# Clearing a stage's semaphores by ranges of neighbouring numbers in a two-layer hybrid trunk

## The chip, the cores and the metric

One core of one Trainium2 chip runs the whole program. The metric is the device time in microseconds, 4389.47 us as the median of 3 runs (4385.0 to 4389.6). The profiled execution was a further one.

## What is computed

The reference is a trunk of DEPTH = 2 layers over 256 latent and 256 context tokens of width 1024, in f32. Cut to its frame, one layer is:

```
mod_l = silu(c) @ w_mod[l] + b_mod[l]
hl = rmsnorm(x, norm1_w[l]) * (1 + sc1) + sh1
pl_ssd, pl_rwkv, pl_na, pl_gate = split(hl @ w_in[l])
ya, yb, yc = ssd_mixer(...), rwkv_mixer(...), na_mixer(...)
x = x + g1 * merge_branches((ya, yb, yc), pl_gate, w_branch[l], w_out[l])
toks = rmsnorm(x, norm2_w[l]) * (1 + sc2) + sh2
x = x + g2 * moe_ffn(toks, route_hierarchical(toks, ...), ...)   # 4 groups of 4 experts, top 2
```

The context tokens go through the same weights; in the second layer (l = 1) they are only read. A last rmsnorm gives the output, 256 x 1024. The change touches none of this arithmetic: it touches the semaphores between the stages.

## The kernel before, in words

The program is a chain of 21 stages, each written by hand as one block with a program for every engine: PE (TensorE), DVE (VectorE), ACT (ScalarE), POOL (GpSimd) and SP (SyncE, which issues nearly all DMAs). Activations stay in SBUF, channels on the partitions and tokens in the free dimension, 512 tokens in layer 0 and mostly the 256 latent ones in layer 1. Each layer runs, in this order, `modulation` (w_mod streamed through five buffers), `conv_project` (z/x/B/C projection and convolution), `ssd_mix`, `branch_streams` (z, attention, two merges), `rwkv_heads`, `residual_out` (w_out), `norm_tokens`, `route`, `experts_rows` (layer 0) or `experts` (layer 1), and `experts_dense` (runs only when a token found no slot, so here it reads a flag and ends). `finish` closes the program.

A block ends in a barrier of all engines: each engine drains and adds to a semaphore, POOL collects them and lets all five go on. A stage's semaphores come from the context manager `phase` (L164), entered ahead of the block, so its end stands behind the block's barrier. There SP alone clears them, one `sem_clear` each (L170), and there is no barrier after that. The numbers go back to the allocator one stage later, when another barrier lies between (L171 to 173). So the other engines go straight into the next stage, and SP goes into it behind its clears. SP's clears are in front of whatever SP does first in the next stage:

- `conv_project` (L516, L517): two small DMAs, then `take_first_slabs`.
- `branch_streams` and `residual_out`: `take_first_slabs` at once. It waits for the two weight slabs that the stage before had already asked for (the ring holds two slabs of 2 MB) and then hands each on by an increment (L229). PE's first matmul (L264 in `multiply_slabs`, L1014 in `branch_streams`) waits for that increment and not for the DMA itself.
- `modulation` (L301): the first DMA of w_mod.
- `rwkv_heads` (L1444, L1445, L1440): the weights of the low-rank terms and of the next turn; PE itself starts on weights that an earlier stage loaded (L1480).
- `norm_tokens`: the first six DMAs of the experts' down weights. `route`, `experts_rows`, `experts`, `experts_dense`, `finish` and `ssd_mix`: SP first waits for something that the stage works out later, or does nothing.

Two places have a second barrier. At the end of each layer's experts the stage's semaphores are cleared, then 19 (layer 0) or 14 (layer 1) semaphores of the weight stream one by one (L2908), and then all engines meet in a barrier (L2909). At the very end 15 long-lived semaphores are cleared (L2913) ahead of the last barrier (L2914).

The numbers are handed out in ascending order, from the one behind the last given, from 255 on to 114, and past those still held. In the program before, the stages have these (the number of semaphores, then the ranges):

```
layer 0                              layer 1
modulation     22  114-135           modulation     22  214-235
conv_project    6  136-141           conv_project    6  236-241
ssd_mix        30  142-171           ssd_mix        30  114-129, 242-255
branch_streams 43  172-214           branch_streams 43  130-148, 164-187
rwkv_heads     76  114-148, 215-255  rwkv_heads     76  149-163, 188-248
residual_out    6  168-173           residual_out    6  121-126
norm_tokens     5  174-178           norm_tokens     5  127-131
route           9  179-187           route           9  132-140
experts_rows    9  188-196           experts        13  141-148, 168-172
experts_dense  17  197-213           experts_dense  17  166-167, 173-187
                                     finish          7  159-165
```

That is 457 semaphores in 27 ranges over the 21 stages.

Of the kernel before, what the change touches and what calls it, by code (L numbers as in the profile page):

```python
# [162 lines left out]
@contextmanager  # L163
def phase(nc, names):  # L164

    _phase[0] += 1
    sems = namedtuple("Semaphores", names)(*(nc.alloc_semaphore(name=f"{n}_{_phase[0]}") for n in names.split()))
    yield sems
    for s in sems:
        nc.sync.sem_clear(s)  # L170
    for s in _cleared:  # L171
        nc.release_semaphore(s)
    _cleared[:] = sems
# [96 lines left out]
def modulation(k):  # L270
# [4 lines left out]
    NR = 5  # L275
    with ExitStack() as st:
        s = st.enter_context(phase(nc, " ".join(f"slab{i}" for i in range(NR)) + " slab_free rows_done rows_in turned rows_free padded silu_c small rest vec "
                               "tokens updated square summed mean normed affine"))
        sc = st.enter_context(nc.sbuf_tensor(f"silu_c{l}", [P, KT, 32], F32))
# [136 lines left out]
def norm_tokens(k, t0, *cleared):  # L416

    nc, l = k.nc, k.layer
    n = TT - t0
    with ExitStack() as st:  # L420
        s = st.enter_context(phase(nc, "sum root scaled moved cleared"))
        rinv = st.enter_context(nc.sbuf_tensor(f"rinv_second{l}", [P, TT], F32))
        block = st.enter_context(nc.Block())
# [32 lines left out]
def residual_out(k, t0):  # L456

    nc, l = k.nc, k.layer
    with ExitStack() as st:
        s = st.enter_context(phase(nc, STREAM + " updated square summed"))  # L460
        sq = st.enter_context(nc.sbuf_tensor(f"sq_out{l}", [P, 2, TT], F32))
        block = st.enter_context(nc.Block())
# [2504 lines left out]
```

How the kernel before makes its waits and increments, by code:

```python
    def settle(self):  # L147
        self.eng.wait_ge(self.sem, self.base + self.n)
# [37 lines left out]
def inverse_root(k, act, rinv, sums, done):  # L186
    k.nc.scalar.activation(rinv, sums, ACT.Ln, scale=1.0 / D, bias=const(k, "eps")).then_inc(done, 1)
    act.wait_ge(done, 1)
    k.nc.scalar.activation(rinv, rinv, ACT.Exp, scale=-0.5).then_inc(done, 1)
# [26 lines left out]
def take_first_slabs(k, sp, loaded, amount):  # L217
    plan = k.plans.pop(0)
    if not k.asked:
        for h in range(2):
            for dst, src in slab_parts(k, plan, h):
                sp.dma_start(dst, src).then_inc(k.first[h], 16)
    k.n_first += 16 * len(slab_parts(k, plan, 0))
    k.asked = False
    for h in range(2):
        sp.wait_ge(k.first[h], k.n_first)
        sp.sem_inc(loaded[h], amount)
# [2 lines left out]
def ask_next_slabs(k, sp, frees):  # L232
    if not k.plans:
        return
    for h in range(2):
        sp.wait_ge(*frees[h])
        for dst, src in slab_parts(k, k.plans[0], h):
            sp.dma_start(dst, src).then_inc(k.first[h], 16)
    k.asked = True
# [2 lines left out]
def load_slabs(k, sp, s, w, col0, turns):  # L243
    wv = w.rearrange("(kt p) c -> p kt c", p=P)
    loaded = (s.loaded0, s.loaded1)
    take_first_slabs(k, sp, loaded, 16)
    for n in range(2, 2 * turns):
        sp.wait_ge(s.tile_done, 4 * (n - 1))
        sp.dma_start(k.ring[:, n % 2], wv[:, :, col0 + 512 * n:col0 + 512 * n + 512]).then_inc(loaded[n % 2], 16)
    ask_next_slabs(k, sp, [(s.tile_done, 8 * turns - 4), (s.tile_done, 8 * turns)])
```

## Time and profile before

| | us |
|---|---|
| median of 3 runs | 4389.47 |
| lowest and highest run | 4385.0, 4389.6 |
| profiled execution, its time | 4385.84 |
| profiled execution, first to last instruction (span) | 4384.1 |

In the profile PE is busy for 4005.9 us of the span (91%), DVE for 1383.7 (32%), ACT for 1013.4 (23%) and POOL for 455.3 (10%). "Busy" leaves out register, semaphore and DMA-issuing instructions; those stand as an engine's queue (SPq, PEq and so on). SP has no busy time at all and is seen only in its queue. Each row of work gives the idle time ahead of it on its engine and, behind an arrow, what ended that idle time. All times below count from the span's start.

### The profile page before, as it was taken

To read this page: it belongs to the slowest core of one execution; us is meant where nothing else is said; L and a number is where in the kernel's file an instruction comes from. 1 tells how busy PE (TensorE), PEld (TensorE's weight loads), DVE (VectorE), ACT (ScalarE), POOL (GpSimd) and SP (SyncE) were. 2 spreads that over 40 slices of the span, in tenths; PEclk is the share of its full clock that TensorE was granted. 3 is DMA by queue.
4 is the path that set the end of the run, shared out by engine and by line. 5 is a ranking of instruction groups with operands and counts; after the bars stand their busy time and mean duration, and the time that the engine had idled before them with its cause. 6 is when DMAs were issued, how large, how long until landed. Compare 5 with 4: busy or idle time off the path is not lost. (4 is left out here: it accounts for less than half of the span.)

```text
span 4384.1 us, 94494 instructions
## 1 busy us (share of the span) xinstructions
PE 4005.9 (91%) x42596; PEld 2712.0 (62%) x42596; DVE 1383.7 (32%) x2784; ACT 1013.4 (23%) x1735; POOL 455.3 (10%) x360
## 2 busy tenths in 40 slices
PE   5999998999999999879999588998999999998996
PEld 2454445448887785368878235656678887874332
DVE  1471004235555461110000145202255555512111
ACT  2121005124343331100000122103143443311101
POOL 0050002101111110000000002102011111100000
PEclk8999999999999999979999798999999999998998
DMA  7201222220000011349998631223201000146996
GB/s 306 77 1 58 86 62 64 96 57 19 19 19 19 21 42 40 140 166 315 324 309 285 247 136 39 87 77 106 79 19 35 19 19 21 42 138 255 404 403 269
DMA packets 299414, 539.20 MB, mean 123 GB/s; under 512 B 52320, under 2 KB 160112, under 8 KB 298880
## 3 DMA queue, kind: packets, MB, share of 16 engines
q1 hardware_dynamic: 291392, 505.80, 33.4%
q0 software_dynamic: 7616, 27.27, 1.7%
q8 instruction: 342, 5.60, 0.5%
q14 instruction: 64, 0.52, 0.0%
HBM read 515.13 MB, written 17.87 MB: 122 GB/s over the span
## 5 line engine op out<-in xcount | busy, mean ns | idle before, releaser
L1470 PE MATMUL bank<-inv 64*64 64x64 f32 x15104 | 487.9, 219 | 19.0 <-ACT inv L1793 8.5
L1470 PEld LDWEIGHTS bank<-inv 64*64 64x64 f32 x15104 | 467.4, 135 | 56.5 <-issue 54.7
L1014 PE MATMUL bank<-sb_h,sb_ring 128*128 128x512 f32 (+1 forms) x1344 | 480.4, 517 | 14.3 <-DMA sb_ring<-w_branch 7.0
L1014 PEld LDWEIGHTS bank<-sb_h,sb_ring 128*128 128x128 f32 x1344 | 257.8, 193 | 230.2 <-issue 198.3
L2665 PEld LDWEIGHTS bank<-xs,gu 128*128 128x128 f32 x3072 | 347.3, 193 | 8.6 <-issue 7.4
L2665 PE MATMUL bank<-xs,gu 128*128 128x96 f32 x3072 | 347.3, 276 | 1.0 <-DVE hid L2594 1.0
L1480 PE MATMUL bank<-sb_h,sb_ring 128*128 128x512 f32 (+1 forms) x672 | 276.8, 566 | 6.2 <-DMA sb_ring<-w_in 4.1
L264 PE MATMUL bank<-sb_h,sb_ring 128*128 128x512 f32 x512 | 224.7, 602 | 17.4 <-SPq L229 17.4
L1480 PEld LDWEIGHTS bank<-sb_h,sb_ring 128*128 128x128 f32 x672 | 128.7, 193 | 138.5 <-issue 129.3
L264 PEld LDWEIGHTS bank<-sb_h,sb_ring 128*128 128x128 f32 x512 | 98.8, 193 | 141.7 <-issue 124.2
L2490 PE MATMUL bank<-gu,xs 128*64 128x512 f32 x768 | 169.8, 594 | 9.0 <-DMA gu<-moe_w_up 8.5
L1014 PE MATMUL bank<-sb_branch,sb_ring 128*128 128x512 f32 (+1 forms) x512 | 170.5, 486 | 0.0
L2677 PE MATMUL bank<-sb_ring,hid 128*96 128x512 f32 x384 | 167.5, 592 | 1.2 <-issue 1.2
L2593 DVE TENSOR_TENSOR hid<-hid,bank 128x192 f32<-128x192 f32 x16 | 5.7, 355 | 510.9 <-ACT hid L2629 510.9
L1793 ACT ACTIVATE inv<-bank 128x512 f32<-128x512 f32 x192 | 111.3, 596 | 155.9 <-PE bank L1470 155.9
L1237 DVE TENSOR_TENSOR sb_acc<-zs,bank 128x512 f32<-128x512 f32 (+1 forms) x16 | 8.9, 554 | 430.5 <-PE bank L1014 430.5
L1014 PEld LDWEIGHTS bank<-sb_branch,sb_ring 128*128 128x128 f32 x512 | 97.1, 190 | 69.3 <-issue 61.2
L363 PE MATMUL bank<-mod_ring,silu_c 128*32 128x512 f32 x384 | 68.2, 847 | 69.2 <-DMA mod_ring<-w_mod 69.2
L2490 PEld LDWEIGHTS bank<-gu,xs 128*64 128x64 f32 x768 | 53.5, 137 | 119.6 <-issue 99.7
L2677 PEld LDWEIGHTS bank<-sb_ring,hid 128*96 128x96 f32 x384 | 61.3, 163 | 95.7 <-issue 95.7
L1470 PE MATMUL bank<-cc,bb 64*64 64x128 f32 x2048 | 118.7, 269 | 0.1
L1086 PE MATMUL bank<-vtok,pt 128*128 128x64 f32 x640 | 86.2, 275 | 30.6 <-DVE sb_branch L1277 23.3
(391 smaller groups left out, 5939.6 us busy)
## 6 DMA issues: line engine op xcount, KB each, us to landing
mod_ring<-w_mod SPq DMA_DIRECT2D x24, 2048.0 KB, 22.7
sb_ring<-w_in SPq DMA_DIRECT2D x24, 2048.0 KB, 7.8
gu<-moe_w_gate SPq DMA_DIRECT2D x128, 384.0 KB, 8.7
gu<-moe_w_up SPq DMA_DIRECT2D x128, 384.0 KB, 10.0
sb_ring<-moe_w_down SPq DMA_DIRECT2D x96, 512.0 KB, 4.5
gu<-moe_w_gate SPq DMA_DIRECT2D x64, 768.0 KB, 14.0
gu<-moe_w_up SPq DMA_DIRECT2D x64, 768.0 KB, 14.9
sb_ring<-moe_w_down SPq DMA_DIRECT2D x32, 1024.0 KB, 14.8
```

The source lines that it names most:

```text
L264: mm = nc.tensor.matmul(banks[j], ring[:, h, kt, P * j:P * j + P], rhs[:, kt], start=kt == 0, stop=kt == KT - 1)
L363: mm = nc.tensor.matmul(k.bank[1 + j % 4][32 * g:32 * g + 32], sc[:, 4 * hf + g], ring[:, n % NR, g, 512 * i:512 * i + 512], start=hf == 0 ...
L1014: mm = nc.tensor.matmul(out, left(kt), right(kt), start=kt == 0, stop=kt == KT - 1)
L1086: mm = nc.tensor.matmul(Y[u % 2][:, 64 * h:64 * h + 64], pt[:, j % 3, t], vtok[:, t, P * f + 64 * h:P * f + 64 * h + 64], start=t == 0, st ...
L1237: tt(k.acc[:, t, t0:], sg[:, t % 2, t0:], projs[0][t % 2][:, 0:n], ALU.mult).then_inc(s.merged, 1)
L1470: m = mm(bank[hs, at:at + w], left(hs), right(hs), start=start, stop=True, skip_group_check=True)
L1480: m = mm(k.bank[RAW_BANK[j]][:, WHOLE[j]:], w[:, j, kt], k.h[:, kt, WHOLE[j]:], start=kt == 0, stop=kt == KT - 1)
L1793: ac(slot(z, into), eight(k.bank[2 + 3 * z + j]), ACT.Copy).then_inc(s.ev_a, 1)
L2490: m = mm(wide[i][rows[e], :], xs[:, kt, rows[e]], cols[:, 512 * i:512 * i + 512], start=kt == 0, stop=kt == KT - 1)
L2593: nc.vector.tensor_tensor(h[:, 0:2 * C], h[:, 0:2 * C], wide[1][:, 2 * C:4 * C], ALU.mult)
L2665: m = mm(wide[j // 4][:, C * (j % 4):C * (j % 4) + C], w[:, P * j:P * j + P], xs[:, kt], start=kt == 0 and j % 4 == 0, stop=kt == KT - 1, ...
L2677: m = mm(outs[half][0:C], hid[:, r % 2, f], ws.down[d % ws.n_down][:, 0, 512 * half:512 * half + 512], start=f == 0, stop=f == HT - 1)
```

## The change

When a stage ends, its semaphores' numbers are sorted, split into runs of neighbouring numbers, and each run is cleared by one `sem_clear` with a range. Nothing else is changed: the same engine clears, at the same place, and numbers are released as before. The clears at L2908 and L2913 stay one by one.

```diff
     yield sems
-    for s in sems:
-        nc.sync.sem_clear(s)
+    numbers = sorted(s.num for s in sems)
+    for i, a in enumerate(numbers):
+        if i == 0 or numbers[i - 1] + 1 < a:
+            first = a
+        if i + 1 == len(numbers) or a + 1 < numbers[i + 1]:
+            nc.sync.sem_clear(range(first, a + 1))
     for s in _cleared:
         nc.release_semaphore(s)
     _cleared[:] = sems
```

## Rows read from the trace of the kernel before

**Rows 1.** Who waited for whom: us in total, times, longest us.

```profile
PE bank L363 <- DMA mod_ring<-w_mod: 69.2, 24, 16.8
PE bank L264 <- SPq L229: 29.7, 4, 8.9
PE bank L1014 <- SPq L229: 5.9, 2, 3.2
...
SPq L2811 <- DVE sb_h L2845: 11.5, 4, 9.5
```

**Rows 2.** Line 170: count, ns min/median/max, first and last start; whole, then stretches.

```profile
L170 SPq EVENT_SEMAPHORE_RANGE_CLEAR  x457: 25/30/49, 88.7 to 4382.9; - x153
...
L170 SPq EVENT_SEMAPHORE_RANGE_CLEAR  x76: 25/28/30, 3919.8 to 3924.1; - x76
...
L170 SPq EVENT_SEMAPHORE_RANGE_CLEAR  x76: 25/30/37, 1784.6 to 1789.4; - x76
...
L170 SPq EVENT_SEMAPHORE_RANGE_CLEAR  x30: 25/30/49, 338.2 to 340.4; - x30
...
L170 SPq EVENT_SEMAPHORE_RANGE_CLEAR  x22: 25/30/39, 88.7 to 90.0; - x22
```

**Rows 3.** Timeline into conv_project: start us, us, engine, line [idle before <-releaser].

```profile
90.05 0.37 SPq L516 DMA_DIRECT2D wdt<-w_in  x1
90.47 0.57 SPq L517 DMA_DIRECT2D dtpar<-dt_par  x1
...
91.15 1.22 PE L264 MATMUL bank<-sb_h,sb_ring 128*128 128x512 f32 x1 [8.44 <-SPq L229]
```

**Rows 4.** Timeline into residual_out of layer 0.

```profile
1783.67 0.69 DVE L2154 TENSOR_TENSOR sb_acc<-sb_acc,bkt 128x512 f32<-128x512 f32 x1
...
1789.48 2.93 PE L264 MATMUL bank<-sb_acc,sb_ring 128*128 128x512 f32 x3 [6.64 <-SPq L229]
...
1790.83 0.37 SPq L2347 DMA_DIRECT2D wr<-router_w  x1
```

**Rows 5.** GB/s in 40 slices of 1740 to 1800 us, 1.5 us each.

```profile
GB/s 348 197 0 0 0 0 5 0 0 0 0 0 0 0 0 33 371 395 407 193 0 0 0 0 0 0 0 0 0 105 411 390 396 112 38 52 214 395 412 414
```

**Rows 6.** Timeline into branch_streams of layer 0.

```profile
338.24 1.28 ACT L1150 ACT_TABLE_LOAD   x1 [10.03 <-PEq L563]
...
340.52 1.22 PE L1014 MATMUL bank<-sb_h,sb_ring 128*128 128x512 f32 x1 [3.21 <-SPq L229]
```

**Rows 7.** Timeline into modulation of layer 1.

```profile
2472.93 0.93 SPq L301 DMA_DIRECT2D mod_ring<-w_mod  x2
```

**Rows 8.** Line 2909, the barrier behind the experts.

```profile
L2909 DVEq DRAIN  x2: 19/19/19, 2465.2 to 4360.7; - x2
...
L2909 SPq DRAIN  x2: 7/7/7, 2466.7 to 4362.2; - x2
```

**Rows 9.** Timeline into rwkv_heads of layer 0, SP and PE.

```profile
924.88 0.58 SPq L1444 DMA_DIRECT2D sb_ring<-wa  x1
...
922.23 8.80 PE L1480 MATMUL bank<-sb_h,sb_ring 128*128 128x512 f32 x16 [2.02 <-PEq L918]
930.96 0.69 PE L1489 MATMUL bank<-sb_ring 64*128 64x512 f32 x1
```

**Rows 10.** Stretches: us, PE busy (x), PEld, DVE, ACT, POOL, PEclk, DMA share, GB/s.

```profile
340.50:346.70 6.20, 6.18 (x8) 2.58 (x9) 0.00 (x0) 0.00 (x0) 1.25 (x1) 0.50 0.00 0
...
1789.40:1793.90 4.50, 4.42 (x5) 1.85 (x6) 0.00 (x0) 0.00 (x0) 0.00 (x0) 0.50 0.47 75
...
2773.90:2776.90 3.00, 2.97 (x7) 2.44 (x8) 0.00 (x0) 0.00 (x0) 1.77 (x1) 0.50 0.00 0
...
3924.20:3927.20 3.00, 2.96 (x7) 2.43 (x8) 0.00 (x0) 0.00 (x0) 0.00 (x0) 0.50 0.48 178
...
923.50:926.90 3.40, 3.40 (x5) 1.35 (x4) 0.86 (x9) 0.00 (x0) 0.00 (x0) 0.50 0.13 38
```

**Rows 11.** GB/s in 40 slices of 3930 to 4000 us, 1.75 us each.

```profile
GB/s 388 406 410 409 400 402 404 402 400 402 355 25 0 0 0 108 405 396 424 421 410 412 417 405 213 5 0 0 0 0 9 5 0 0 0 0 0 0 49 342
```

## Prediction

> **What bounds the kernel now.** I read the waits first, since PE is busy for 91% of the span and only what moves PE, or what PE waits for, moves the end. In the table of waits PE waits 29.7 us in four places at L264 and 5.9 us in two at L1014 for "SPq L229" [rows 1]. That is SP's increment that hands on a weight slab. Slabs take long to come, so one would expect PE to be waiting for a DMA there. It isn't: in residual_out of layer 0 the transfer rate shows two bursts of about 2 MB, one in slices 15 to 19 (1762 to 1770 us), one in slices 29 to 33 (1783 to 1791) [rows 5]. The first slab was there some 13 us before the stage began. What SP does between the barrier and L229 is to clear: 76 clears from 1784.6 to 1789.4 [rows 2], and PE's first matmul starts at 1789.48 behind 6.64 us of idle time, while the last work of the stage before, on DVE, ended at 1783.67 + 0.69 = 1784.4 [rows 4]. So of the 6.6 us, 4.8 are SP's clears. SP is never "busy" in the page, and still it sets PE's start at six borders.
>
> The other numbers that matter are those of a clear itself. All 457 are already instructions of the range kind, here with a range of one; each is shown for 25 to 49 ns, 30 at the median [rows 2]. From the 76 clears of layer 1 (3919.8 to 3924.1), 4.3 us / 75 = 57 ns from one to the next, so 57 ns is what one costs SP [rows 2]. In layer 0 some runs are longer than that: 4.8 instead of 4.3 us for 76, and 2.2 instead of 29 x 0.057 = 1.7 us for 30 [rows 2], about 1.0 us of stalls in sum, whose cause no row names.
>
> **The change, part by part.** 457 clears become 27, so 430 go, 430 x 0.057 = 24.5 us of SP's time. What counts is where SP is waited for. No instruction is added on any other engine, no wait is added, and what SP is queued up to do comes earlier.
>
> (a) Into conv_project, twice: 22 clears become 1, 21 x 0.057 = 1.2 us each. Behind them SP issues two DMAs (0.37 and 0.57 us) and reaches L229; PE starts at 91.15 [rows 3]. Late next would be the two issues, which stay. 2.4 us.
>
> (b) Into branch_streams, twice: 30 become 1 in layer 0 and 2 in layer 1 (29 + 28) x 0.057 = 3.2 us. PE starts at 340.52, just behind the last clear at 340.4 [rows 2, 6]. ACT's table load, 338.24 to 339.52, doesn't hold PE, and its first copy comes only after a group of matmuls [rows 6].
>
> (c) Into residual_out, twice: 76 become 2, 2 x 74 x 0.057 = 8.4 us, the largest term. Late next in layer 0: SP's wait for the second slab, which lands at 1790.8 whatever SP does (its next issue, at 1790.83, shows it [rows 4]); PE needs it only half way through the stage, behind the four output tiles of the first slab. The rates show that the first slab landed long before [rows 5].
>
> (d) The barrier behind the experts: SP drains at 2466.7, DVE had at 2465.2, so all wait for SP's clears [rows 8]. 9 become 1 and 13 become 2: 19 x 0.057 = 1.1 us. The 19 and 14 stream clears stay.
>
> (e) Into modulation of layer 1: 17 become 1, 16 x 0.057 = 0.9 us. SP's first DMA of w_mod at 2472.93 is behind them [rows 7], and PE waits 69.2 us for these slabs over both layers [rows 1], so the stage is set by the stream and moves with its start.
>
> (f) Ahead of the last barrier 7 become 1: 6 x 0.057 = 0.3 us.
>
> (g) 142 further clears go at no gain. Into rwkv_heads 43 become 1 and 2 (83 in all): SP's first DMA leaves at 924.88, but PE is in 8.80 us of matmuls on weights already there and goes on at 930.96 without a gap [rows 9]; without that cover it would be worth 2.4 us a layer. Into ssd_mix, norm_tokens, route and the experts 44 go, where SP has nothing that anyone waits for at once, and into finish 15, where SP waits for DVE's last line anyway [rows 1]. Were all of this uncovered it would be 142 x 0.057 = 8.1 us; I take 0.
>
> The sum of (a) to (f) is 42 + 57 + 148 + 19 + 16 + 6 = 288 clears, 288 x 0.057 = 16.5 us. Of the 1.0 us of stalls, both on gated borders, between 0 and 1.0 may go with the clears; I take 0.5.
>
> (h) TensorE's clock. Behind these borders PE starts at a granted clock of 0.50, which is 1.2 of 2.4 GHz: 6.2 and 3.0 us into branch_streams, 4.5 and 3.0 us into residual_out [rows 10]. Half speed costs half of that, (6.2 + 4.5 + 3.0 + 3.0) / 2 = 8.3 us in sum. The idle time ahead would shrink from 3.2 to 1.0 us and from 6.6 to 2.0 in layer 0, and alike in layer 1. The nearest row for a short gap is the one into rwkv_heads: 2.02 us idle, and the clock still fell, for 3.4 us, which cost 1.7 [rows 9, 10]. If all four borders came to cost as that one, 8.3 - 6.8 = 1.5 us are won; if none fell, 8.3. For residual_out, whose gaps come nearest to that row, I take its price (3.75 - 3.4 = 0.3 us won); for branch_streams, with gaps of half that length, half of the 4.6 us. Together 2.6 us. Into conv_project the gap stays above 7 us and the clock stays low.
>
> Sum: 16.5 + 0.5 + 2.6 = 19.6 us. Against the profiled execution's own 4385.84 us that gives 4366.2. That execution was 3.6 us below the median of the runs (4389.47), near the lowest of them; against the median it is **4369.9 us**, which I give.
>
> **What a range costs.** The trace has no range of more than one number. Bounded by rows: at the low end a range takes the 57 ns of a single clear whatever its length; at the high end the 30 ns for which a clear is shown are spent once per number, and only the other 27 are saved. I take the low end, because the instruction is the same one and a range of one uses it in full. The Trainium skill speaks for the high end (Runtime: NRT & Kernel Launch, "The ~15µs preamble/postamble breakdown"): the runtime's reset of 51 semaphores per engine is put at about 1.5 us, 29 ns a number, though it doesn't say whether single or ranged clears do it. By that figure, as an estimate, the saving at the gated borders would be about half; no row of this case shows it.
>
> **Rivals.** *A range works through its numbers.* 288 x 0.027 = 7.8 us are won, 4381.7 us. For it: a clear is shown as working for 30 of its 57 ns, and that part would be the one to grow [rows 2]. Against it: nothing in the rows varies with a number. 10%.
>
> *A stream takes the gain back.* The experts of layer 1 live on their weight stream. If it ran through from residual_out on, its start (behind the second slab's landing, which doesn't move) would set the end, and the 4.2 us of that border would be lost: 4374 us. Against it: the rates pause from about 3974 to 3996 us, with the buffers full, until the experts free some [rows 11]; an earlier start just shortens the pause. 6%.
>
> *Slower.* The place is the same borders: if one number inside a range cost more than the 57 ns of a clear of its own, each border would be longer than before. The gated borders hold 302 numbers in 14 ranges. From 57 ns a number it decides; at 90 ns, say, (90 - 57) x 302 = 10 us slower, 4399 us. Nothing in the rows speaks for it. 3%.
>
> That the change doesn't do what it says could come from numbers that aren't neighbours; the table of numbers gives at most two ranges a stage, so no more than a few clears are in doubt. 1%, about no change.
>
> **How the numbers follow.** The forecast holds 80%. A measurement of this kernel can tell about 0.2%, 8.8 us, from no change. Forecast and stream case lie beyond that (86%, and a little of the first rival when clock luck is added), the first rival mostly within. Range: the low end is 16.5 + 1.0 + 8.3 = 25.8 us below the median, 4363.7, less some 2.5 us as the runs before themselves reach 4.5 below theirs: 4361. The high end takes in the first rival: 4382.
>
> **What would show it.** In the changed profile line 174 should have 27 clears; PE's waits for SP's increment should fall from 35.6 us to about 21 (247 of the 288 clears stand there: 35.6 - 14.1 - 0.5), with the first matmul of residual_out under 2.5 us behind the last matmul ahead of it. If a clear of 41 numbers is shown for far more than 30 ns, the first rival is right, above 2.4 us the slower one. If the waits fall as said but the time doesn't, the stream took it, and the experts' waits for DMA grow. If the clock still stands at 0.50 for as long into branch_streams, term (h) was wrong.

## The result, and the profile after

The changed kernel ran in 4363.28 us (median of 4 runs, 4361.85 to 4364.93), beside 4388.43 us for the kernel before in the same comparison. The ratio is 0.9944, 95% interval 0.9927 to 0.9961: 24.6 us faster, between 17 and 32. In a later series of its own (e9 below) the ratio was 0.9961, 0.9947 to 0.9975: 17 us, between 11 and 23. The profiled execution took 4361.85 us, its span was 4360.0. Forecast were 4369.9 us and 19.6 us of gain.

The clears of the changed kernel, line 174, over the whole span and then at some borders (count, ns min/median/max, first and last start in us):

```profile
L174 SPq EVENT_SEMAPHORE_RANGE_CLEAR  x27: 31/49/125, 89.6 to 4358.7; - x27
...
L174 SPq EVENT_SEMAPHORE_RANGE_CLEAR  x1: 68/68/68, 89.6 to 89.6; - x1
L174 SPq EVENT_SEMAPHORE_RANGE_CLEAR  x1: 75/75/75, 337.8 to 337.8; - x1
L174 SPq EVENT_SEMAPHORE_RANGE_CLEAR  x1: 98/98/98, 916.4 to 916.4; - x1
L174 SPq EVENT_SEMAPHORE_RANGE_CLEAR  x2: 83/92/101, 1781.3 to 1781.4; - x2
L174 SPq EVENT_SEMAPHORE_RANGE_CLEAR  x2: 49/87/125, 3903.9 to 3904.0; - x2
L174 SPq EVENT_SEMAPHORE_RANGE_CLEAR  x1: 35/35/35, 208.4 to 208.4; - x1
```

27 clears stand where 457 stood [rows 2]. The rows also tell what a range costs: it is shown for 35 ns with 6 numbers, 68 with 22, 75 with 30 and 98 with 43. From 6 to 43 numbers that is 63 ns more, so 1.7 ns a number, beside the 30 ns for which a clear of one number is shown. By that rate the 302 numbers on the gated borders cost about half a microsecond in sum.

Who waited for whom, PE, in the changed kernel, beside [rows 1]:

```profile
PE bank L268 <- SPq L233: 18.3, 4, 7.4
...
PE bank L2531 <- DMA down<-moe_w_down: 16.9, 13, 1.5
...
PE bank L2494 <- DMA gu<-moe_w_up: 6.8, 8, 1.1
...
PE bank L1018 <- SPq L233: 2.2, 2, 1.1
```

The waits for SP's increment fell from 35.6 to 20.5 us, by 15.1. Of the 18.3 that remain at L268, 14.7 (7.25 and 7.40) are the two borders into conv_project, where PE has been idle since well before the barrier.

The timeline at the borders of layer 0, into conv_project, branch_streams and residual_out, beside [rows 3, 6, 4], and the first DMA of modulation in layer 1, beside [rows 7]:

```profile
89.68 0.37 SPq L520 DMA_DIRECT2D wdt<-w_in  x1
...
90.79 2.08 PE L268 MATMUL bank<-sb_h,sb_ring 128*128 128x512 f32 x2 [7.25 <-SPq L233]
...
337.92 1.56 PE L1018 MATMUL bank<-sb_h,sb_ring 128*128 128x512 f32 x3 [1.08 <-SPq L233]
...
1780.30 0.69 DVE L2158 TENSOR_TENSOR sb_acc<-sb_acc,bkt 128x512 f32<-128x512 f32 x1
...
1781.57 8.85 PE L268 MATMUL bank<-sb_acc,sb_ring 128*128 128x512 f32 x20 [2.11 <-SPq L233]
...
2461.70 1.61 SPq L305 DMA_DIRECT2D mod_ring<-w_mod  x2
```

Into residual_out PE now starts 0.6 us behind DVE's last instruction (1780.99); before it was 5.1 us. And the row, which merges matmuls that follow one another, has changed its look: 20 matmuls in 8.85 us, 0.44 us each, where the first three of before took 2.93 us [rows 4]. That is the clock. Stretches of the changed kernel, the same borders (us, PE busy, PEld, DVE, ACT, POOL, PEclk, DMA share, GB/s), beside [rows 10]:

```profile
337.90:341.00 3.10, 3.08 (x7) 1.44 (x8) 0.00 (x0) 1.15 (x1) 3.10 (x1) 1.00 0.04 8
...
1781.60:1786.00 4.40, 4.40 (x11) 2.01 (x12) 0.00 (x0) 0.00 (x0) 0.00 (x0) 1.00 1.04 399
...
2759.70:2762.70 3.00, 3.00 (x14) 2.66 (x15) 0.00 (x0) 1.01 (x1) 3.00 (x1) 1.00 0.01 3
...
3904.20:3908.00 3.80, 3.77 (x17) 3.34 (x18) 0.01 (x1) 0.00 (x0) 0.00 (x0) 1.00 0.98 370
...
914.50:916.60 2.10, 0.08 (x2) 0.04 (x1) 1.38 (x2) 0.00 (x0) 0.00 (x0) 1.00 0.03 7
916.60:921.00 4.40, 4.40 (x7) 1.95 (x8) 1.94 (x9) 0.00 (x0) 0.00 (x0) 0.63 0.62 161
```

All four borders that began at 0.50 now begin at a granted clock of 1.00. The one into rwkv_heads, whose price was taken for a short gap, fell again (0.63 over the 4.4 us behind it). The span shortened by 4384.1 - 4360.0 = 24.1 us. PE's earlier starts are 15.1 of it, the four half-clock stretches 8.3 (their cost in [rows 10]), which leaves 0.7 for the rest; the barriers and the stream of term (d) to (f) were forecast at 2.3. That rest also holds what two executions differ by anyway.

The neat sum hides larger pieces of both signs. A stage's length can be read from the moment at which one barrier lets DVE go to the moment at which the next one does. Measured so, the two branch_streams and the two residual_out are together 21.9 us shorter (the table below), both conv_project 2.9 us, modulation of layer 1 2.3 us, and the three stretches that end in the barriers behind line 2908 and at the very end 1.2 us. Against that, the two rwkv_heads are 3.5 us longer and ssd_mix of layer 1 2.3 us longer, though the change does nothing inside them. In ssd_mix of layer 1 the same 426 matmuls took longer, at a lower granted clock; before and after:

```profile
2670.90:2772.09 101.19, 83.41 (x426) 60.64 (x426) 61.53 (x101) 18.90 (x32) 31.17 (x24) 0.85 0.02 8
...
2655.86:2759.36 103.50, 86.78 (x426) 62.65 (x426) 61.51 (x101) 18.78 (x32) 31.16 (x24) 0.81 0.02 7
```

PE's busy time over the whole span fell by 5.0 us (4005.9 to 4000.9) and not by 8.3: part of what the clock gives at the four borders was lost elsewhere in this execution. The 8.3 us are the clock's share at those borders, not over the whole program.

### The profile page after: what moved, and what is told of

Same layout as the page of the kernel before. It is cut to its first block and busy times, and to the rows that moved or that the text cites. A ratio compares the mean times of both kernels' runs of the same rounds, so it can differ in the third digit from the quotient of the medians.

```text
span 4360.0 us, 94064 instructions
## 1 busy us (share of the span) xinstructions
PE 4000.9 (92%) x42596; PEld 2710.7 (62%) x42596; DVE 1384.2 (32%) x2784; ACT 1013.2 (23%) x1735; POOL 455.7 (10%) x360
## 5 line engine op out<-in xcount | busy, mean ns | idle before, releaser
L268 PE MATMUL bank<-sb_h,sb_ring 128*128 128x512 f32 x512 | 224.4, 601 | 14.6 <-SPq L233 14.6
L268 PEld LDWEIGHTS bank<-sb_h,sb_ring 128*128 128x128 f32 x512 | 98.7, 193 | 138.9 <-issue 124.1
## 6 DMA issues: line engine op xcount, KB each, us to landing
mod_ring<-w_mod SPq DMA_DIRECT2D x24, 2048.0 KB, 22.4
```

What stands on the lines that cost most here:

```text
L268: mm = nc.tensor.matmul(banks[j], ring[:, h, kt, P * j:P * j + P], rhs[:, kt], start=kt == 0, stop=kt == KT - 1)
```

## The experiments

All ratios are to the kernel before, in the same series. Series of kernel before: 4384.44 us (e1 to e4, 20 runs), 4386.38 us (e5 to e8, 31 runs), 4386.28 us (e9 to e11, 9 runs). Times of one kernel spread over 10 us and more within a series, so that a few microseconds show in a profile's rows before they show in a ratio. The lengths of the four stages behind the borders into branch_streams and residual_out, in us (from barrier to barrier, as above), one profiled execution each:

| kernel | branch_streams, layer 0 | residual_out, layer 0 | branch_streams, layer 1 | residual_out, layer 1 | sum |
|---|---|---|---|---|---|
| before | 583.80 | 65.04 | 387.30 | 35.69 | 1071.8 |
| the change | 578.64 | 58.32 | 382.86 | 30.12 | 1049.9 |
| e2, ranges into residual_out | 583.84 | 58.31 | 386.09 | 30.12 | 1058.4 |
| e3, clears on POOL | 578.54 | 58.07 | 382.68 | 29.88 | 1049.2 |
| e5, PE busy in residual_out | 582.16 | 62.86 | 383.62 | 34.22 | 1062.9 |
| e6, PE busy in all four | 580.77 | 62.86 | 385.24 | 34.22 | 1063.1 |
| e7, 18 clears put back | 579.73 | 61.52 | 386.66 | 32.75 | 1060.7 |
| e8, 36 clears put back | 583.95 | 61.97 | 386.45 | 35.02 | 1067.4 |

Branch_streams of layer 1 is the least steady of them: the kernel of e4 and e10, the same program twice, took 387.83 and 383.18 us there.

**e1, ranges only where nobody waits for SP.**

```diff
-    for s in sems:
-        nc.sync.sem_clear(s)
+    hidden = _phase[0] in (2, 4, 6, 7, 8, 12, 14, 16, 17, 18, 20)
+    if hidden:
+        numbers = sorted(s.num for s in sems)
...
+    else:
+        for s in sems:
+            nc.sync.sem_clear(s)
```

> Ranges only behind the stages after which nobody waits for SP (the 11 borders of term (g): into ssd_mix, rwkv_heads, norm_tokens, route, experts and finish); the 288 clears of the gated borders stay one by one. 142 clears fewer, 8.1 us of SP's time. Theory (what counts is who waits for SP): no change, 0 within 4 us, and PE's waits for SP's increment stay near 35.6 us. Rival (fewer instructions of SP help by themselves, through its fetching or anything else shared): about 142/430 of the 25 us gained, 8 us faster.

Measured: ratio 1.0003, 0.9994 to 1.0012 (4386.79 us), so between 3 us faster and 5 us slower. PE's waits for SP's increment are 35.9 us in its profile (29.3 + 6.6):

```profile
PE bank L273 <- SPq L238: 29.3, 4, 8.6
...
PE bank L1023 <- SPq L238: 6.6, 2, 3.3
```

The rival's 8 us lie outside the interval. 142 clears fewer are worth less than 3 us, and nothing that the waits show, where other work covers them.

**e2, ranges only on the two borders into residual_out.**

```diff
+    if names.startswith("w_in second_in"):
+        numbers = sorted(s.num for s in sems)
...
+    else:
+        for s in sems:
+            nc.sync.sem_clear(s)
```

> Ranges only behind rwkv_heads, that is on the two borders into residual_out, 148 clears fewer. Theory with the clock: 8.5 us for the clears (0.5 of it stalls) and 3.7 us for TensorE's clock, which no longer falls to half behind these borders: 12.2 us faster than before. Rival without the clock: 8.5 us. In the profile PE's first matmul stands 0.4 us behind the barrier and the stage shows no stretch at a clock of 0.50.

Measured: ratio 0.9973, 0.9963 to 0.9983, 11.8 us faster (between 7.5 and 16). The point is the theory's with the clock, 12.2, though 8.5 lies within the interval too. The profile decides: the two residual_out stages are 6.7 and 5.6 us shorter, 12.3 in sum, and PE starts with a full-speed row behind a gap of 2.10 us,

```profile
1785.08 2.41 PE L272 MATMUL bank<-sb_acc,sb_ring 128*128 128x512 f32 x5 [2.10 <-SPq L237]
```

five matmuls in 2.41 us where the kernel before took 2.93 for three [rows 4]. About half of the 24.6 us sits on these two borders.

**e3, the same 457 single clears, issued by POOL.**

```diff
     for s in sems:
-        nc.sync.sem_clear(s)
+        nc.gpsimd.sem_clear(s)
```

> The 457 clears stay one by one, but POOL issues them in place of SP. Theory (SP's place on the path counts, not the number of clears): nearly the whole gain of the change, 23 to 25 us, less about 0.5 us where POOL's gathers in experts_rows now stand behind 9 clears and 1 us at the barriers behind the experts. Rival (the number of clears counts, whoever issues them): no change from before.

Measured: ratio 0.9949, 0.9937 to 0.9960, 22.4 us faster (between 17.5 and 27.6). The clears are all there, line 170, now on POOL and shown for 44 ns each, and PE doesn't wait for them (19.6 us of waits for SP's increment are left, 20.5 in the change; the four stages are as short as there):

```profile
L170 POOLq EVENT_SEMAPHORE_RANGE_CLEAR  x457: 44/44/48, 87.6 to 4365.1; - x153
...
1778.75 1.55 PE L264 MATMUL bank<-sb_acc,sb_ring 128*128 128x512 f32 x3 [1.86 <-SPq L229]
```

So neither the number of clears nor the range as such is the cause of the gain. The cause is that the clears stood in the queue of the engine that lets PE go.

**e4, ranges also for the stream's and the last semaphores.**

```diff
-                for sem in k.stream.sems:
-                    nc.sync.sem_clear(sem)
+                clear(nc, k.stream.sems)
...
-        for sem in (k.dt_in, k.w3_in, *k.first, *k.pool_dma):
-            nc.sync.sem_clear(sem)
+        clear(nc, (k.dt_in, k.w3_in, *k.first, *k.pool_dma))
```

> The changed kernel with the stream's 19 and 14 and the last 15 semaphores cleared by ranges too; 45 clears fewer, all ahead of a barrier at which everyone waits for SP. Theory: 45 x 0.058 = 2.6 us faster than the change, 27 to 28 us faster than before. Rival (a longer range costs with its numbers as much as the clears it replaces): no faster than the change.

Measured: ratio 0.9941, 0.9928 to 0.9953, 25.9 us faster (between 21 and 32). 48 clears became 4 here (44 fewer, not the 45 of the text), 31 in all. The ratios can't tell it from the change; the barriers can. Drains at the barrier behind the experts, DVE and SP, first and last start in us: the change, then this kernel (its execution in e10).

```profile
L2913 DVEq DRAIN  x2: 19/19/19, 2455.2 to 4337.6; - x2
L2913 SPq DRAIN  x2: 7/7/7, 2456.3 to 4338.5; - x2
...
L2916 DVEq DRAIN  x2: 19/19/19, 2457.1 to 4340.1; - x2
L2916 SPq DRAIN  x2: 7/7/7, 2457.2 to 4340.3; - x2
```

SP now drains 0.1 and 0.2 us behind DVE, where it was 1.1 and 0.9 in the change. From barrier to barrier the three closing stretches take 1.25 us in sum in e4 and e10, 3.88 in the change and in e9: 2.6 us less, which is what the theory has.

**e5 and e6, all clears kept, and PE kept busy in the gap.** This takes the clock's share apart from SP's. In e5 the matmuls stand in residual_out alone; e6 adds those of branch_streams.

```diff
         def _(pe):
+            for i in range(5 if t0 == 0 else 9):
+                nc.tensor.matmul(k.bank[7][:, t0:], const(k, "ones"), k.acc[:, i % KT, t0:], start=True, stop=True)
             multiply_slabs(pe, nc, s, k.ring, k.acc[:, :, t0:], banks, 1, s.updated)
...
+            for i in range(2 if t0 == 0 else 3):
+                nc.tensor.matmul(k.bank[7][:, t0:], const(k, "ones"), k.h[:, i, t0:], start=True, stop=True)
             gate_z()
```

> The kernel before with all its clears, and in residual_out PE runs matmuls whose result nobody reads (5 in layer 0, 9 in layer 1, about 4 us) while it waits for SP; they write a bank that the stage doesn't use. SP's path is that of before. Theory (the idle gap lets the clock fall, and that is a loss of its own beside the clears): 3.3 us in layer 0 and 1.7 us in layer 1 won, 4 to 5 us faster than before, with no stretch at 0.50 behind these borders. Rival (the clock is no separate term): no change, or slower by what the matmuls overrun the wait.

> As e5, and in branch_streams too (2 and 3 such matmuls ahead of the first wait). Theory: another 3.4 us in layer 0 and 1.5 us in layer 1, so 8 to 10 us faster than before with every clear in its old place, the clock's whole share of the change's 25 us. Rival: as e5.

Measured: e5 0.9986, 0.9977 to 0.9995, 6.1 us faster (between 2 and 10); e6 0.9980, 0.9971 to 0.9989, 8.8 us faster (between 5 and 13). The timeline of e5 into residual_out of layer 0 and a stretch of it, then stretches of e6 into branch_streams:

```profile
1782.74 4.53 PE L473 MATMUL bank<-sb_acc,sb_consts 128*128 128x512 f32 x10 [1.84 <-PEq L1390]
1787.54 4.99 PE L264 MATMUL bank<-sb_acc,sb_ring 128*128 128x512 f32 x11 [0.27 <-SPq L229]
...
1782.60:1789.40 6.80, 6.39 (x15) 2.72 (x16) 0.00 (x0) 0.00 (x0) 0.00 (x0) 1.00 0.79 297
```

```profile
338.40:345.00 6.60, 6.12 (x14) 2.68 (x15) 0.00 (x0) 1.28 (x1) 3.51 (x1) 1.00 0.02 5
2768.90:2775.00 6.10, 5.79 (x26) 4.83 (x27) 0.09 (x1) 1.67 (x2) 3.51 (x1) 1.00 0.01 4
```

PE waits for SP as long as ever, but with work in hand, and the real matmuls start at full speed. e6 gains 8.8 us without one clear less, which agrees with the 8.3 us of the four half-clock stretches in [rows 10]; its four stages are 8.7 us shorter than before. In e5 the two residual_out stages are 3.7 us shorter, of the 4 to 5 expected.

**e7 and e8, the change with the delay put back in doses.** 18 (e7, shown) or 36 (e8) clears of one already cleared semaphore on the four borders into branch_streams and residual_out.

```diff
             nc.sync.sem_clear(range(first, a + 1))
+    if names.startswith(("w_in second_in", "logits act")):
+        for _ in range(18):
+            nc.sync.sem_clear(sems[0])
```

> The changed kernel with 18 more clears of one already cleared semaphore on the four borders into branch_streams and residual_out. Each such border is 18 x 0.058 = 1.0 us longer. Theory: 4.2 us slower than the change where the clock stays up, and up to 6.8 us more where gaps of 2 to 3 us let it fall; by the gaps (about 2.1 and 2.4 us in branch_streams, 3.1 and 2.4 us in residual_out) I expect the clock to fall in one or two of the four, 6 to 8 us slower. Rival (a clear costs SP nothing that PE sees): no change.

> As e7 with 36 clears, 2.1 us on each of the four borders, gaps of 3.2 to 4.2 us, as long as those of before in branch_streams. Theory: 8.4 us for the clears and the clock falling on all four, 5 to 8 us: 13 to 16 us slower than the change. Rival without the clock: 8.4 us.

Measured: e7 0.9972, 0.9962 to 0.9982 (12.3 us faster than before); e8 0.9978, 0.9969 to 0.9987 (9.6 us). Against the change, whose two series give 24.6 and 17.1 us, that is 5 to 12 and 7 to 15 us slower; the ratios don't separate the theory from its rival, as the change's own spread is too wide. The rows do. In e8 the gaps ahead of the four borders are 8.7 us longer in sum than in the change, and the four stages 17.5 us longer. The rival without the clock has nothing for the other 8.8 us. The whole is a little more than the 13 to 16 us expected. In e7 the gaps are 5.1 us longer and the stages 10.7, where 6 to 8 were expected. Its timeline shows the gap ahead of the four borders (in brackets), and the stretches behind them the clock:

```profile
338.76 1.56 PE L1021 MATMUL bank<-sb_h,sb_ring 128*128 128x512 f32 x3 [2.17 <-SPq L236]
...
1784.06 4.54 PE L271 MATMUL bank<-sb_acc,sb_ring 128*128 128x512 f32 x6 [3.61 <-SPq L236]
...
2764.51 2.07 PE L1021 MATMUL bank<-sb_h,sb_ring 128*128 128x256 f32 x4 [2.60 <-SPq L236]
...
3911.36 2.08 PE L271 MATMUL bank<-sb_acc,sb_ring 128*128 128x256 f32 x4 [2.63 <-SPq L236]
```

```profile
338.70:342.00 3.30, 3.23 (x8) 1.56 (x9) 0.00 (x0) 0.10 (x1) 2.33 (x1) 1.00 0.01 2
1784.00:1789.00 5.00, 4.94 (x8) 2.16 (x9) 0.00 (x0) 0.00 (x0) 0.00 (x0) 0.66 0.75 282
2764.50:2768.00 3.50, 3.49 (x9) 2.84 (x10) 0.00 (x0) 0.00 (x0) 1.84 (x1) 0.55 0.01 2
3911.30:3916.00 4.70, 4.64 (x14) 3.86 (x15) 0.00 (x0) 0.00 (x0) 0.00 (x0) 0.66 0.98 373
```

Behind 2.17 us the clock stayed up (1.00), behind the other three it fell. I had expected one or two to fall. In e8, with gaps of 3.34, 4.24, 3.29 and 3.71 us, all four started low:

```profile
339.10:344.00 4.90, 4.87 (x6) 2.19 (x7) 0.00 (x0) 0.00 (x0) 1.12 (x1) 0.50 0.01 2
1786.00:1790.00 4.00, 3.98 (x6) 1.89 (x7) 0.00 (x0) 0.00 (x0) 0.00 (x0) 0.61 0.74 275
2769.60:2773.00 3.40, 3.40 (x8) 2.78 (x9) 0.00 (x0) 0.00 (x0) 1.13 (x1) 0.50 0.00 0
3916.80:3922.00 5.20, 5.16 (x12) 4.17 (x13) 0.00 (x0) 0.00 (x0) 0.00 (x0) 0.50 0.67 253
```

**e9 to e11, the change, all ranges, and a warm start of conv_project, in one series.** e9 is the change, e10 is e4. e11 adds to e10, at the end of PE's part of modulation:

```diff
             pe.sem_inc(s.turned, 1)
+            for i in range(4):
+                nc.tensor.matmul(k.bank[7], const(k, "ones"), k.ssq[:], start=True, stop=True)
```

> The changed kernel once more, in one series with e10 and e11, so that all three are compared with the same runs of before. 24 to 25 us faster than before, as at first (16.4 for PE's starts, the barriers and the stream, about 8 for the clock).

> The kernel of e4 beside the change itself: 45 clears of 60 ns in four ranges or fewer, all ahead of barriers where SP comes last, so 2.4 us faster than e9.

> The kernel of e10, and PE runs four matmuls whose result nobody reads at the end of modulation, where it is idle for some 6 us while DVE and ACT finish. Theory: conv_project starts at 1.00 in place of 0.50; that stretch is 5 us after the change, in both layers, so about 2.5 us each, 5 us faster than e10. Rival: the matmuls hold the barrier up or the clock falls all the same: no gain.

Measured: e9 0.9961, 0.9947 to 0.9975 (4369.52 us, 4359.64 to 4372.70); e10 0.9939, 0.9925 to 0.9952 (4362.35 us); e11 0.9930, 0.9917 to 0.9944 (4356.29 us). The expected 2.4 us between e9 and e10 and 5 us between e10 and e11 are of the right sign in the ratios (9.6 and 4 us), and neither is clear of the intervals; for e10 the closing barriers show the 2.6 us (under e4). e11's border into conv_project of layer 0 is won as meant, at full clock; the stage took 116.71 us, and 119.56 in e10:

```profile
81.60 5.37 PE L388 MATMUL bank<-ssq_first,sb_consts 128*128 128x512 f32 x8
88.68 2.84 PE L272 MATMUL bank<-sb_h,sb_ring 128*128 128x512 f32 x6 [1.72 <-SPq L237]
...
88.70:95.00 6.30, 6.30 (x15) 2.94 (x16) 0.00 (x0) 0.00 (x0) 0.00 (x0) 1.00 0.15 25
2532.00:2539.00 7.00, 6.63 (x12) 2.90 (x13) 0.39 (x1) 0.00 (x0) 0.00 (x0) 0.76 0.14 23
```

In layer 1 PE was idle for 3.56 us behind its extra matmuls, and the start wasn't won: 0.76 over the first 7 us. e11 is the fastest of all kernels here; that it beats the change itself rests on a 13 us difference of medians within the series, 0.9944 at its upper end against 0.9947 at the change's lower end.

## Why the prediction was right

The forecast of 19.6 us lies between the two series of the change (24.6 and 17.1 us), and both medians lie in the range. The mechanism is as forecast. That the number lies between the two is in part luck: one term is 5.7 us too small at its own borders, and some stages that the forecast leaves alone came out longer in the profiled execution. By its steps:

- That SP sets PE's start at six borders and not a slab's landing: right. e3 is the proof by another way, since it moves the clears and keeps them all.
- Terms (a) to (c), 247 clears at 57 ns and half of the stalls, 14.6 us: measured 15.1 in PE's waits. In single borders of layer 0: 8.44 to 7.25 us into conv_project (1.2 forecast, 1.2 measured), 3.21 to 1.08 into branch_streams (1.7 and up to 0.5 of stalls forecast, 2.1 measured), 6.64 to 2.11 into residual_out (4.2 and up to 0.5 forecast, 4.5 measured). So most of the 1.0 us of stalls went, not half; what had caused them stays open. Into conv_project the earlier start was not all kept: in layer 0 the stage became 0.5 us shorter for 1.2 us of earlier start, since PE ran at 0.50 for 4.4 us behind it in place of 2.9; in layer 1 it became 2.5 us shorter for 1.5.
- Terms (d) to (f), 2.3 us: right where they stand, by the rows. At the barrier behind the experts SP drains 1.1 and 0.9 us behind DVE (the rows under e4) in place of 1.5 and 1.5 [rows 8], 1.0 us less in sum, where 1.1 was forecast. The first DMA of modulation in layer 1 leaves 0.15 us behind the barrier (2461.70 and 2461.55) in place of 1.1 (2472.93 and 2471.80), 1.0 us earlier, where 0.9 was forecast. The last stretch is 0.2 us shorter, where 0.3 was forecast. That only 0.7 us of the span is left for them comes from the stages that grew.
- Term (g), nothing for the 142 covered clears: right, e1.
- Term (h), the clock, 2.6 us: this is the term that was mis-sized. It is worth 8.3 us by [rows 10] where all four falls vanish, as they did in both profiles of the change (here and in e9); e6 measures 8.8 us (5 to 13) with the clears kept. The step that failed is the choice of the nearest row: "2.02 us idle, and the clock still fell" was taken as the price of both gaps into residual_out, and half of the low clock's cost was left standing in branch_streams; measured, none of either stayed. Behind the same gap of 2.02 us into rwkv_heads the clock fell again in the changed kernel, while behind 2.11 us into residual_out, 1.08, 1.14 and 1.56 us elsewhere and 2.17 us in e7 it did not. And that one row was no fixed price: in the 13 profiles the clock fell behind this gap in 9 and not in 4 (e3, e5, e10, e11). The range had held it, through its lower end (all 8.3 us).
- What a range costs: near the low bound. 1.7 ns a number are 0.5 us over 302 numbers. The first rival would have had 30 ns a number, the slower rival over 57. The sign given for the first rival, a clear of 41 numbers "shown for far more than 30 ns", was worded too loosely: 43 numbers are shown for 98 ns, three times 30, and still the rival, which needs 43 x 30 = 1290 ns, is out. The Trainium skill (Runtime: NRT & Kernel Launch, "The ~15µs preamble/postamble breakdown") puts the runtime's reset of 51 semaphores per engine at about 1.5 us. The 29 ns a number worked out from that, an estimate, don't hold for ranges in this trace; they are near the 30 ns for which a single clear is shown.
- The stream rival: PE's waits for the experts' down weights in layer 1 (L2527 before, L2531 after) went from 18.1 to 16.9 us and those for the up weights from 8.5 to 6.8, in place of growing by the 4 us of the border.
- One reading of rows is off without harm: the first slab's burst ends at about 1770 [rows 5] and the stage begins at 1784.6, so the slab was there between 14 and 15 us ahead, not 13.

## What to carry to other kernels

Housekeeping behind a barrier, semaphore clears above all, is paid by whoever waits for the first thing that the clearing engine does next: look at what starts late at each border, not at how many instructions an engine has. Clear by ranges, or let an engine clear that nobody waits for; both gave about the same here. Where a wait of PE is shortened from some 3 to 7 us to 1 or 2, count the half-speed start behind it as a gain of its own: here 8.3 us at the borders, beside 15.1 us of waits. And read the effect of such a change stage by stage; the whole span adds what the clock did elsewhere.

## What the runs showed of the hardware that was not expected

- A clear of a range is shown for 35 ns with 6 numbers and 98 ns with 43, about 1.7 ns a number; a clear of one number costs SP 57 ns from start to start, and on POOL is shown for 44 ns instead of 30.
- The clock after a short gap is no matter of the gap's length alone. The gap of 2.02 us into rwkv_heads of layer 0 comes ahead of the same matmuls in every kernel, and the clock fell in 9 of 13 profiles. In e4 and e10, which are the same program, it fell once and stayed up once. Gaps of 2.10 and 2.11 us into residual_out left it up in all 6 profiles that have them, 2.17 us in e7 too; behind 2.60 us and more it fell at all these borders. What decides it is open. Below, e4 and then e10: the 4.4 us into rwkv_heads of layer 0, and branch_streams of layer 1 as a whole.

```profile
915.90:920.30 4.40, 4.38 (x7) 2.01 (x8) 1.93 (x9) 0.00 (x0) 0.00 (x0) 0.64 0.59 162
2755.35:3143.18 387.83, 365.82 (x1522) 255.42 (x1522) 58.32 (x198) 76.81 (x164) 44.48 (x17) 0.97 0.31 93
...
915.60:920.00 4.40, 4.37 (x11) 2.01 (x12) 1.93 (x9) 0.00 (x0) 0.00 (x0) 1.00 0.59 153
2762.21:3145.39 383.18, 360.90 (x1522) 251.87 (x1522) 58.41 (x198) 76.88 (x164) 44.50 (x17) 0.99 0.32 94
```

- An unchanged program spreads over some 10 us in a longer series (4380.28 to 4390.56 for the kernel before, 31 runs), and the change over 13 (4359.64 to 4372.70). The lines above show one way to it: the same 1522 matmuls of branch_streams in layer 1 took 4.9 us more, at a granted clock of 0.97 in place of 0.99, in the same program. In the five runs of e9, time and mean granted clock go together (4359.64 us at 0.960, 4364.50 at 0.959, 4369.52 at 0.958, 4371.37 at 0.957, 4372.70 at 0.956). In the 31 runs of the kernel before they don't: its fastest, 4380.28, has 0.954. So the clock explains part of the spread, and how much is not shown. Both profiles of the change come from the fastest run of their series, so how the four borders look in its slower runs isn't known.
